# Seven block products for eight in the down projection of a transformer layer, in pairs of output tiles

## The reference

```python
f = rmsnorm(x, g_ffn_pre)
g_, u_ = jnp.split(f @ w_gate_up, 2, axis=-1)
x = x + rmsnorm((jax.nn.silu(g_) * u_) @ w_down, g_ffn_post)
```

## Time and profile before

| | us |
|---|---|
| median of 3 runs (769.42 to 770.26) | 769.75 |
| the profiled execution, its own time | 768.84 |
| its span | 766.7 |
| TensorE busy | 757.5 (99%) |
| VectorE / ScalarE / GpSimd busy | 484.2 / 357.0 / 70.5 |

### The profile page before, as it was taken

One profiled execution on the slowest core, in us unless ns is written; L12 is line 12 of the kernel. 1 busy time (PEld: TensorE's weight loads), 2 busy tenths in 40 slices (PEclk: granted clock), 3 DMA queues, 4 the chain that ended last, 5 costly groups with the idle time before them and its releaser, 6 DMA issues.

```text
span 766.7 us, 16315 instructions
## 1 busy us (share of the span) xinstructions
PE 757.5 (99%) x5954; PEld 718.4 (94%) x5954; DVE 484.2 (63%) x760; ACT 357.0 (47%) x627; POOL 70.5 (9%) x156
## 2 busy tenths in 40 slices
...
GB/s 263 169 110 117 162 131 139 128 104 135 129 134 104 61 74 168 175 70 181 160 194 6 106 109 109 109 108 81 85 109 109 55 127 138 107 91 111 93 91 127
DMA packets 196979, 91.68 MB, mean 120 GB/s; under 512 B 65143, under 2 KB 190539, under 8 KB 196941
## 3 DMA queue, kind: packets, MB, share of 16 engines
...
q0 software_dynamic: 2576, 6.45, 2.5%
...
HBM read 82.37 MB, written 6.81 MB: 116 GB/s over the span
## 4 chain that ended last, share of the span: by engine, by line
PE 97%; DMA 1%; POOL 1%; DVE 0%; DVEq 0%; issue 0%; ACT 0%; POOLq 0%
PE ps L975 34%; PE ps L1364 28%; PE ps L1428 17%; PE ps L1258 6%; PE ps L1332 3%; PE ps L1181 2%; PE ps L1082 1%; PE ps L1096 1%; PE ps L1114 1%; DMA strow<-in_state_h_dram 1%; PE ps L1156 1%; PE ps L1266 1%; PE ps L1067 1%; PE ps L1127 1%; POOL prow L833 0%; PE ps L1293 0%
## 5 line engine op out<-in xcount | busy, mean ns | idle before, releaser
L2021 DVE TENSOR_TENSOR w_lo<-w_raw,w_hi 128x1024 fp32r<-128x1024 f32 (+1 forms) x65 | 77.3, 1190 | 120.5 <-ACT w_hi L1501 120.2
L1501 ACT ACTIVATE w_hi<-w_raw 128x1024 fp32r<-128x1024 f32 (+1 forms) x66 | 67.8, 1029 | 122.2 <-PE ps L1428 78.1
L975 PE MATMUL ps<-xin_hi,w_hi 128*128 128x272 f32 x544 | 117.0, 296 | 0.0
L975 PE MATMUL ps<-xin_hi,w_lo 128*128 128x272 f32 x544 | 112.5, 288 | 0.0
L975 PE MATMUL ps<-xin_lo,w_hi 128*128 128x272 f32 x544 | 112.3, 288 | 0.0
L975 PEld LDWEIGHTS ps<-xin_hi,w_hi 128*128 128x128 f32 x544 | 84.8, 188 | 8.1 <-issue 7.6
L975 PEld LDWEIGHTS ps<-xin_lo,w_hi 128*128 128x128 f32 x544 | 85.4, 188 | 0.0
L975 PEld LDWEIGHTS ps<-xin_hi,w_lo 128*128 128x128 f32 x544 | 85.0, 189 | 0.0
L1428 PE MATMUL ps<-hid_hi,w_hi 128*128 128x272 f32 (+2 forms) x352 | 75.3, 289 | 0.0
L1428 PE MATMUL ps<-hid_lo,w_hi 128*128 128x272 f32 (+2 forms) x352 | 74.9, 287 | 0.0
L1428 PE MATMUL ps<-hid_hi,w_lo 128*128 128x272 f32 (+2 forms) x352 | 74.9, 287 | 0.0
...
## 6 DMA issues: line engine op xcount, KB each, us to landing
w_raw<-in_w_in_dram SPq DMA_DIRECT2D x68, 256.0 KB, 3.2
g_raw<-in_w_gate_up_dram SPq DMA_DIRECT2D x40, 256.0 KB, 3.7
w_raw<-in_w_down_dram SPq DMA_DIRECT2D x40, 256.0 KB, 2.8
u_raw<-in_w_gate_up_dram SPq DMA_DIRECT2D x20, 256.0 KB, 3.0
e_raw<-in_w_gate_up_dram SPq DMA_DIRECT2D x20, 256.0 KB, 4.2
...
wo_raw<-in_w_out_dram SPq DMA_DIRECT2D x12, 256.0 KB, 4.0
```

The source lines that it names most:

```text
L975: mm = e.matmul(ps[:, bank + h, 0:HT], wt[:, kw, :], xt[:, kx, h * HT:h * HT + HT], start=first and wt is wh and xt is xh, stop=last and ( ...
L1501: e.activation((to or w_hi[s])[:, 0:k, :], w_raw[s][:, 0:k, :], ACT.Copy).then_inc(hi_done, count)
L2021: e.tensor_tensor(wl[:, 0:k, :], w_raw[s][:, 0:k, :], wh[:, 0:k, :].bitcast(F32), ALU.subtract).then_inc(lo_done, count)
```

## The change

Output tiles 1 to 6 are made in three pairs (n = 0, 1, 2). For 10 of the 22 K tiles (6 to 10, KA, and 11 to 15, KB) the product of a pair is seen as 2 x 2 blocks of 5 K tiles by 128 columns of the weights and 5 K tiles by 272 columns of hid, and made of seven block products with sums of weights (`op_sums`, four per pair) and sums of hid (`hs`, four in all, with high and low parts of their own). The other 12 K tiles stay plain, in four parts of 3 K tiles. So a pair has 15 products, `OP_A11` to the last `OP_P2`, in the order A11, A12, A22, four plain (tile 2n+1), S2, S3, S1, S4, four plain (tile 2n+2); the plain parts sum into the banks of the block results. Each has an operand buffer of three (`op_hi`, `op_lo`, index j % 3); ScalarE may fill one when product j - 3 is done. The weights of the pairs are loaded by GpSimd (four loads of 320 KB and eight of 192 KB a pair, one DMA each, with two buffers for the plain ones), all four weight sums stand ahead of the low parts of the plain products. Snapshots of PSUM (`snap`) and adds on VectorE (`c_11`, `c_21_part`, `c_12`, `c_22_21`) put the results together in SBUF (`c_pair`), from where `y_pair` takes them as `y_evacuate` did. Tiles 0 and 7 are made as before; the chunks of tile 7 are loaded by SyncE, two during the last pair, the third behind the moves of tile 5. The residual rows are loaded in the last pair.

The diff, cut to its core (not shown: addresses, the semaphores' new names, `snap`, `hs_high`, `hs_low` and the bodies of the adds; `op_high` is one ScalarE copy, `op_low` one VectorE subtraction):

```diff
+SK, KA, KB = 5, 6, 11
+PLAIN_K, PK = (0, 3, 16, 19), 3
+N7 = (KD - 2) // 2
+OPS7 = 15
+(OP_A11, OP_A12, OP_A22, OP_P1, OP_S2, OP_S3, OP_S1, OP_S4, OP_P2) = (0, 1, 2, 3, 7, 8, 9, 10, 11)
+C_LAST = C_DOWN + 3
+HS_0, OP_0, SUM_0, C_0 = 4, KD, 3 * NS, NS
...
+            for n in range(N7):
+                for m in (2 * n - 1, 2 * n):
+                    for part in range(3):
+                        if m >= 0:
+                            move_y(m, m % 2, part)
+            e.wait_ge(op_sum, SUM_0 + 4 * N7)
+            e.wait_ge(op_l, OP_0 + OPS7 * (N7 - 1) + OP_S4 + 1)
+            for c in range(2):
+                k0 = sum(DOWN_K[:c])
+                load(C_LAST + c, (1 + c) % 2, wd[:, k0:k0 + DOWN_K[c], (KD - 1) * P:KD * P], DOWN_K[c])
+            for part in range(3):
+                move_y(KD - 3, 1, part)
+            load(C_LAST + 2, 1, wd[:, KF - DOWN_K[2]:KF, (KD - 1) * P:KD * P], DOWN_K[2])
+            for part in range(3):
+                move_y(KD - 2, 0, part)
...
+            def load_op(n, op, buf, k0, m):
+                e.dma_start(buf[:, :, :], wd[:, k0:k0 + SK, m * P:m * P + P]).then_inc(raw_in[op], 16)
+
+            def load_plain(n, i):
+
+                r = 8 * n + i
+                k0, m = PLAIN_K[i % 4], 2 * n + 1 + i // 4
+                e.dma_start(raw_p[r % 2][:, :, :], wd[:, k0:k0 + PK, m * P:m * P + P]).then_inc(raw_p_in[r % 2], 16)
...
+            e.wait_ge(lo_done, C_DOWN + 4)
+            load_op(0, "11", raw_11, KA, 1)
...
+            load_plain(0, 0)
...
+            load_op(0, "12", raw_12, KB, 1)
+            load_op(0, "22", raw_22, KB, 2)
...
+            load_op(0, "21", raw_21, KA, 2)
+            load_plain(0, 1)
+            for n in range(N7):
+                o = OPS7 * n
+                for i in (2, 3, 4, 5):
+                    e.wait_ge(op_l, OP_0 + o + OP_P1 + i - 1)
+                    load_plain(n, i)
+                if n + 1 < N7:
+                    e.wait_ge(op_sum, SUM_0 + 4 * n + 4)
+                    e.wait_ge(op_l, OP_0 + o + OP_S2 + 1)
+                    load_op(n + 1, "11", raw_11, KA, 2 * n + 3)
+                    e.wait_ge(op_l, OP_0 + o + OP_S3 + 1)
+                    load_op(n + 1, "21", raw_21, KA, 2 * n + 4)
+                    e.wait_ge(op_l, OP_0 + o + OP_S1 + 1)
+                    load_op(n + 1, "22", raw_22, KB, 2 * n + 4)
...
+                for i in (6, 7):
+                    e.wait_ge(op_l, OP_0 + o + OP_P2 + i - 5)
+                    load_plain(n, i)
+                if n + 1 < N7:
+                    for i in (0, 1):
+                        e.wait_ge(op_l, OP_0 + o + OP_P2 + i + 3)
+                        load_plain(n + 1, i)
+
+            e.wait_ge(op_used, OP_0 + OPS7 * (N7 - 1) + OP_S1 + 1)
...
+            e.wait_ge(op_used, OP_0 + OPS7 * N7 - 1)
...
+            def block_product(n, j, bank, x, first, last):
+
+                e.wait_ge(op_l, OP_0 + OPS7 * n + j + 1)
+                wh, wl = op_hi[j % 3], op_lo[j % 3]
+                for k, (xh, xl) in enumerate(x):
+                    for wt, xt in ((wh, xh), (wh, xl), (wl, xh)):
+                        mm = e.matmul(ps[:, bank, 0:HT], wt[:, k, :], xt, start=first and k == 0 and wt is wh and xt is xh,
+                                      stop=last and k == SK - 1 and wt is wl, skip_group_check=True)
+                mm.then_inc(op_used, 1)
...
+                for i, k0 in enumerate(PLAIN_K):
+                    j = j0 + i
+                    e.wait_ge(op_l, OP_0 + OPS7 * n + j + 1)
...
+                    mm.then_inc(op_used, 1)
+
+            for n in range(N7):
+                if n > 0:
...
+                block_product(n, OP_A11, U_BANK, hid_block(KA, 0), True, True)
+                if n > 0:
+                    e.wait_ge(c_done, C_0 + 5 * n - 4)
+                block_product(n, OP_A12, C11_BANK, hid_block(KB, 0), True, False)
+                if n > 0:
+                    e.wait_ge(c_done, C_0 + 5 * n)
+                e.wait_ge(hs_l, HS_0 + 1)
+                block_product(n, OP_A22, C21_BANK, sum_block(3), True, False)
+                if n > 0:
...
+                plain_rest(n, OP_P1, (C11_BANK, C12_BANK), (False, True), (True, False))
+                e.wait_ge(hs_l, HS_0 + 2)
+                e.wait_ge(c_snap, C_0 + 4 * n + 1)
+                block_product(n, OP_S2, U_BANK, sum_block(1), False, True)
+                e.wait_ge(hs_l, HS_0 + 3)
+                block_product(n, OP_S3, C22_BANK, sum_block(2), True, True)
+                e.wait_ge(hs_l, HS_0 + 4)
+                e.wait_ge(c_snap, C_0 + 4 * n + 2)
+                block_product(n, OP_S1, U_BANK, sum_block(0), False, True)
+                block_product(n, OP_S4, C12_BANK, hid_block(KB, 1), False, True)
+                e.wait_ge(c_snap, C_0 + 4 * n + 3)
+                plain_rest(n, OP_P2, (C21_BANK, C22_BANK), (False, False), (True, True))
...
+            e.wait_ge(c_done, C_0 + 5 * N7 - 2)
             down_steps(0, 1, range(DOWN_K[0]), True, False, cut=LAST_CUT).then_inc(tile_done, 1)
...
+            def op_high(n, j):
+
+                o = OPS7 * n + j
+                if o < 2:
+                    e.wait_ge(tile_done, C_DOWN + 4)
+                elif o == 2:
+                    e.wait_ge(tile_done, C_DOWN + 5)
+                else:
+                    e.wait_ge(op_used, OP_0 + o - 2)
...
+            def y_pair(m, s, c, count):
+
+                e.wait_ge(c_done, C_0 + count)
+                e.wait_ge(ysq_used, m + 1)
...
+                e.activation(ysq[:, :], c[:, :], ACT.Square).then_inc(y_free, 1)
...
+            hs_high(3, 4)
...
+            for n in range(N7):
+                if n > 0:
+                    op_high(n, 2); op_high(n, 3)
+                snap(n, 1, OP_A11, c_pair[0][:, 0:HT], 2)
+                if n == 0:
+                    op_high(n, 5)
+                    y_evacuate(0, 0)
+                else:
+                    y_pair(2 * n, 0, c_pair[1], 5 * n)
+                    op_high(n, 4); op_high(n, 5)
+                for j in range(6, 10):
+                    op_high(n, j)
+                snap(n, 2, OP_S2, c_pair[1][:, 0:HT], 2)
+                op_high(n, 10)
+                snap(n, 3, OP_S3, p7_snap[:, :], 5)
+                op_high(n, 11)
+                snap(n, 4, OP_S1, c_pair[1][:, HT:T], 2)
+                op_high(n, 12); op_high(n, 13)
+                y_pair(2 * n + 1, 1, c_pair[0], 5 * n + 3)
+                op_high(n, 14)
+                if n + 1 < N7:
+                    for j in range(2):
...
+            e.wait_ge(op_used, OP_0 + OPS7 * N7 - 1)
+            hi(C_LAST, C_LAST // 2, 1, DOWN_K[0])
+            e.wait_ge(op_used, OP_0 + OPS7 * N7)
+            hi(C_LAST + 1, (C_LAST + 1) // 2, 0, DOWN_K[1])
+            y_pair(KD - 2, 0, c_pair[1], 5 * N7)
+            hi(C_LAST + 2, (C_LAST + 2) // 2, 1, DOWN_K[2])
...
+            e.wait_ge(hid_done, KB + SK)
+            e.wait_ge(a_l, NS)
+            e.tensor_tensor(hs[0][:, :, :], b12, b11, ALU.subtract).then_inc(hs_done, 1)
             up_2(q - 1, 0)
+            e.wait_ge(hs_done, HS_0 + 1)
+            e.tensor_tensor(hs[1][:, :, :], b22, hs[0][:, :, :], ALU.subtract).then_inc(hs_done, 1)
             low_b(q)
             low_c(q, 1)
             gate_1(q, 1)
-            for c in range(2):
-                lo(C_DOWN + c, c)
+            e.wait_ge(c_l, NS)
+            e.tensor_tensor(hs[2][:, :, :], b22, b12, ALU.subtract).then_inc(hs_done, 1)
             up_1(q - 1, 0)
+            lo(C_DOWN, 0)
             low_d(q, 1)
             hid_product(q - 1, hid[:, KF - 2, :])
             for k in range(2):
                 hid_low(k)
+            lo(C_DOWN + 1, 1)
             up_2(q, 1)
-            for k in range(2, EARLY):
+            for k in range(2, 4):
                 hid_low(k)
             up_1(q, 1)
+            e.wait_ge(hs_done, HS_0 + 2)
+            e.wait_ge(d_l, NS)
+            e.tensor_tensor(hs[3][:, :, :], b21, hs[1][:, :, :], ALU.subtract).then_inc(hs_done, 1)
+            for k in range(4, EARLY):
+                hid_low(k)
+            e.wait_ge(hs_done, HS_0 + 4)
+            hid_low(EARLY)
             hid_product(q, hid[:, KF - 1, :])
...
+            def op_sums(n):
+
+                e.wait_ge(raw_in["21"], raw_0["21"] + 16 * n + 16)
+                e.wait_ge(op_l, OP_0 + OPS7 * n + OP_A22 + 1)
+                e.tensor_tensor(raw_22[:, :, :], raw_21[:, :, :], raw_22[:, :, :], ALU.add).then_inc(op_sum, 1)
...
+                e.tensor_tensor(raw_21[:, :, :], raw_11[:, :, :], raw_21[:, :, :], ALU.subtract).then_inc(op_sum, 1)
+                e.wait_ge(op_sum, SUM_0 + 4 * n + 2)
+                e.tensor_tensor(raw_11[:, :, :], raw_22[:, :, :], raw_11[:, :, :], ALU.subtract).then_inc(op_sum, 1)
+                e.wait_ge(op_sum, SUM_0 + 4 * n + 3)
+                e.tensor_tensor(raw_12[:, :, :], raw_12[:, :, :], raw_11[:, :, :], ALU.subtract).then_inc(op_sum, 1)
...
+            def c_11(n):
```

(116 more changed lines are left out.)

129 lines of the change are left out of this document (81 added, 48 removed).

## The result

The changed kernel takes **773.8 us** (median, 771.98 to 774.76) beside 769.2 of the kernel before on the same chips: ratio 1.0051, 95% interval 1.0043 to 1.0059. The forecast was 765.8, range 764.3 to 769.8. The profiled execution took 772.54, 2.14 more than its span, as before; so the spans can be compared: 770.4 against 766.7, 3.7 us.

The account below looks back on a forecast made before the run. TensorE, busy 99% of the span, was taken as the bound. The terms -5.65 + 0.15 + 0.45 + 1.1 + 0.05 = -3.9 gave 764.9 us for the profiled execution, 765.8 for the median, range 764.3 to 769.8.

Parts of the forecast that it names:

- What goes away: In the pairs: 249 matmuls instead of 264 each, so three pairs save 45 x 0.1256 = 5.65 us.
- Start of the pairs: During tile 0: the low part of K tile 7 comes late from VectorE, so TensorE waits 0.15 us.
- A pair, from its first product on: Inside a pair: 31.27 us without gaps; last operand ready at 27.9, due at 29.01, holding to landings of 4.2.
- L: Landing time of GpSimd's weight loads: 3.2 us for 192 KB, 3.6 for 320 KB, bounds 2.4 and 4.7.
- The end, (1): Last tile's start: chunk 0 waits for the second last product's buffers and VectorE's split; TensorE starts 0.45 us late.
- The end, (2), SyncE's queue: Last tile: chunk 2's load stands behind tile 5's twelve moves on SyncE; TensorE waits 1.1 us for it.
- The moves: At the end: tile 6's moves arrive with the first final add and cost at most 0.1; 0.05 summed.
- C: Rival: GpSimd's issue grows with the pieces (1.6 and 2.65 us), delaying operands by 14.5 in all; 778.6 us, chance 0.09.
- D: Rival: the end costs nothing, as SyncE's moves issue faster or tile 5 is ready earlier; 764.7 us, chance 0.09.
- B: Rival: loads land late (4.7 and 5.1) but issue cheaply, delaying operands in every pair; 770.5 us, chance 0.13.

Follow-up runs that it names:

- e3: Against the changed kernel: GpSimd instead of SyncE loads the last tile's chunk 2, and the last operand goes ahead of `y_pair` in the first two pairs; 765.7 us.
- e2: Against the changed kernel: ScalarE makes the last operand's high part ahead of `y_pair` in the first two pairs; 771.7 us.
- e5: e3 with SyncE's load of the last tile's chunk 1 held until the 14th operand is split, and the last operand first in all three pairs; 764.9 us.
- e7: e5 with GpSimd issuing four of the twelve moves of tile 6; 765.2 us.
- e11: e3 with only SyncE's load of the last tile's chunk 1 held until the last pair's 14th operand is split; 766.5 us.
- e8: Against the changed kernel: SyncE loads the last tile's chunk 2 ahead of the moves of tile 5; 773.5 us.
- e10: e8 with chunk 2's low part ahead of the transpose of tile 6 on VectorE; 772.8 us.
- e4: Against the changed kernel: 24 matmuls whose result nobody reads fill TensorE's stall ahead of the last tile's chunk 2; 770.9 us.
- e6: e3 with GpSimd issuing four of the twelve moves of tile 6; 765.6 us.

## Why the prediction was wrong

The forecast had the span 3.9 shorter and it came out 3.7 longer: 7.6 apart. The pairs account for 3.6 of it and the wait for chunk 2 with what follows it for 4.35 (5.45 for 1.1), less 0.3 at the last tile's start. The signs of being wrong that the prediction named both came: landings over 4.2, and TensorE waiting for `op_lo` inside the pairs.

**What goes away**: right. 45 matmuls went, and a pair without gaps takes 31.24 us (e3).

**Start of the pairs**: right. Tile 0 takes 19.78 us (621.61 to 641.39) instead of 19.58, 0.20 for the 0.15 predicted, and TensorE loses it where it was predicted, around 630 (two pairs of matmuls there, at 629.64 and 629.98, take 0.09 and 0.10 longer). All eleven changed kernels show 19.78 or 19.79. That the first pair starts only 0.07 later is chance: tile 0 began at 621.52 to 623.23 in these traces, at 621.74 before, in a part that no edit touches.

**A pair, from its first product on**: wrong, 3.6 us in three pairs where 0 was predicted. The chain was the one described, but the last operand came at 30.8, 29.8 and 29.6 after the pair's start, not at 27.9. The failed term is the path of GpSimd's load of the 7th plain part. The price L was taken as 3.2, and that is right for most (median 3.1, and 3.9 for 320 KB where 3.6 was taken). But this one load comes just behind four block loads (pair 0: 5.19; no run took these away) or beside SyncE's chunks (pair 2: 4.62), over the 4.2 to which the step said it would hold; in pair 1 it landed in 3.31 but was issued 1.8 late. One value for all loads hid that the price is highest where the queue is fullest, which is where this load stands. The text had also named `y_pair` in the chain and not asked whether it must stand ahead of the last operand; e2 shows that it needn't, and that with the operand first the first two pairs get 2.5 us back; their last product then has no gap. What is left in pair 0 is a smaller wait, before S3, which the prediction put at nothing: TensorE starts S3 0.5 late, because its low part came late from VectorE. VectorE is busy for all of 655 to 659, and low parts of two hid sums, 1.57 us each (653.46, 655.68), stand just ahead; no run moved them. The Trainium skill, DMA: Bandwidth & Descriptors, section Anatomy of one DMA, gives 2.5 us for 192 KB, an estimate; no load here was as short (least 2.7).

**The end, (1)**: right mechanism, small. In the changed kernel the late last product hides it: the last tile starts 0.14 after its due time, and the two earlier pairs show 0.12 and 0.11 at the same place. Where no gap stands before the last product (e5, e7, e11) the last pair takes 31.55, which is 0.3 more than 31.24; 0.45 was predicted.

**The end, (2), SyncE's queue**: right mechanism, wrong size: 1.1 predicted, 3.54 measured. Twelve moves took 8.05 (8.3 predicted) and the split 1.86 (1.8). But the moves began 30.4 after the pair's start instead of 28.7, since tile 5 was late, and the load took 4.78 from its first issue to its landing instead of 3.0. The operand was ready 3.1 later in the pair's time than predicted, and TensorE wanted it 0.6 later. The change puts an existing load in another place, and its old price was kept. Why it is slower there stays open: in e8 and e10, where the same two DMAs stand ahead of the moves, they landed 3.6 and 3.9 after the first issue.

**The clock**: absent. A stall was priced at its length; this one cost 1.5 more (e4). The Trainium skill, TensorE: Matmul & The Clock Gate, section HAM oscillation, names idle gaps of TensorE as what brings the clock down. The trace agrees: the clock fell behind the stall of 3.54 and didn't with the stall filled, and the waits of 0.4 to 1.0 us inside the pairs left it at 1.00.

**The moves**, 0.05 predicted: hidden in the changed kernel, because TensorE is later still; once it isn't, the final adds wait 1.90 for them (e3), of which 0.3 (e6) to 0.8 (e7) is seen in the end.

**The rivals.** C is out: an issue took 0.76 and 0.88 (its terms sum to 14.35 at most, where 14.5 stands). D is out: the end lost 5.45. B had the late last operand and was given 0.13, but its premise didn't hold: it had all loads late (4.7 and 5.1, where the medians were 3.1 and 3.9) and the fourth plain operand with them, which never was. It was priced at 770.5, and it too left out the clock. What the prediction said of VectorE and GpSimd side by side rests on less than it says: of the five issues only the last two stood beside the `hid_lo` splits, which start at 628.28. The changed kernel bears it out better: with VectorE busy for all of 655 to 659, the block issues at 656.33 and 658.63 took 0.89 and 0.87, as elsewhere. The forecast added the small terms as if they were independent. They stand on one chain: each late link moved the end, and only there, at the last stall, was the sum paid.
